# Prompt attention of a hybrid decoder step: the two heads of a pair take turns on TensorE, and the copies of the turned probabilities are dealt anew to ScalarE and VectorE

## The reference, cut to what matters

```python
lc = einsum('bqgrd,bcgd->bgrqc', qg, kc) * scale + t5_bias(dist_c)     # compressed keys
o_c = softmax(lc) @ vc
ls = einsum('bqgrd,bgqmd->bgrqm', qg, ks_sel) * scale + bias_s          # selected blocks
o_s = softmax(ls) @ vs_sel
lw = einsum('bqgrd,bkgd->bgrqk', qg, kw) * scale + t5_bias(dist_w)      # window of 512
o_w = softmax(lw) @ vw
o_n = g[0] * o_c + g[1] * o_s + g[2] * o_w
lf = einsum('bqhd,bkhd->bhqk', q_f, kf) * scale + decay                 # FoX
o_f = softmax(lf) @ vf
```

## Time and profile before

| | |
|---|---|
| Runs | 1849.51, 1849.75, 1855.73 us; median 1849.75 |
| Profiled execution | 1857.19 us, of which span 1855.5 us |
| Busy in the span | PE 1732.8 us (93%), DVE 1057.7 (57%), ACT 696.7 (38%), POOL 300.3 (16%) |
| TensorE clock granted, mean | 0.970 of full speed |
| Prompt attention, first scores to last transposes of the outputs | 575.96 to 990.01 us of the span |

### The profile page before, as it was taken

How to read it: one execution, slowest core, us unless ns; L and a number is a source line. 1 busy time by engine, 2 the same in 40 slices (tenths; PEclk the granted TensorE clock), 3 DMA queues, 4 the chain that set the end, 5 groups by cost and what they waited for, 6 DMA issues and landing times. The chain is left out here.

```text
span 1855.5 us, 35458 instructions
## 1 busy us (share of the span) xinstructions
PE 1732.8 (93%) x13557; PEld 1583.8 (85%) x13557; DVE 1057.7 (57%) x2057; ACT 696.7 (38%) x1369; POOL 300.3 (16%) x629
## 2 busy tenths in 40 slices
PE   7999998899885999998898999999999999999998
PEld 6999998776563777777786879999999999999998
DVE  4533332125354777777776557775666664666665
ACT  4110011223232666565666552133333333344343
POOL 3000023500511434353432000000000000000000
PEclk9999999899896999999998999999999999999998
DMA  5548886645999002030201224132222225231112
GB/s 140 185 133 192 223 231 118 221 137 179 309 318 276 2 20 85 1 103 1 92 2 40 93 87 129 58 99 76 70 90 72 70 71 186 103 125 54 46 42 104
DMA packets 145683, 212.64 MB, mean 115 GB/s; under 512 B 23850, under 2 KB 102105, under 8 KB 145459
## 3 DMA queue, kind: packets, MB, share of 16 engines
q1 hardware_dynamic: 113714, 143.36, 24.3%
q0 software_dynamic: 16480, 52.41, 9.3%
q10 hardware_dynamic: 15328, 14.72, 3.3%
HBM read 163.11 MB, written 51.49 MB: 116 GB/s over the span
## 5 line engine op out<-in xcount | busy, mean ns | idle before, releaser
L2108 ACT ACTIVATE probs<-psum,neg_max 128x640 f32<-128x640 f32 (+7 forms) x192 | 138.2, 720 | 115.5 <-DVE neg_max L2256 114.8
L191 PE MATMUL psum<-h_parts,down_hi 128*128 128x352 f32 x528 | 171.7, 325 | 6.0 <-DVE h_parts L3253 4.4
L191 PE MATMUL psum<-x_hi,w_hi 128*128 128x352 f32 x528 | 170.7, 323 | 1.7 <-issue 1.6
L193 PE MATMUL psum<-h_parts,down_lo 128*128 128x352 f32 x528 | 170.5, 323 | 0.0
L192 PE MATMUL psum<-h_parts,down_hi 128*128 128x352 f32 x528 | 170.5, 323 | 0.0
L192 PE MATMUL psum<-x_lo,w_hi 128*128 128x352 f32 x528 | 170.4, 323 | 0.0
L193 PE MATMUL psum<-x_hi,w_lo 128*128 128x352 f32 x528 | 170.3, 323 | 0.0
L191 PE MATMUL psum<-hf_hi,op_hi 128*128 128x264 f32 x576 | 163.5, 284 | 0.6 <-DVE silu L3234 0.6
L193 PE MATMUL psum<-hf_hi,op_lo 128*128 128x264 f32 x576 | 163.5, 284 | 0.0
L192 PE MATMUL psum<-hf_lo,op_hi 128*128 128x264 f32 x576 | 163.3, 284 | 0.0
L2030 PE MATMUL psum<-ident,probs 128*128 128x128 f32 x848 | 139.1, 289 | 8.9 <-ACT probsT L2118 6.1
(11 more groups left out here) (444 smaller groups left out, 4289.6 us busy)
## 6 DMA issues: line engine op xcount, KB each, us to landing
fox_ring<-in_cache_fox_kv SPq DMA_DIRECT2D x128, 256.0 KB, 5.3
zT<-z_stage SPq DMA_DIRECT2D x22, 528.0 KB, 3.9
w_ring<-in_w_in POOLq DMA_DIRECT2D x22, 512.0 KB, 5.7
down_ring<-in_w_ffn_down SPq DMA_DIRECT2D x44, 256.0 KB, 2.7
raw<-in_w_ffn_gate SPq DMA_DIRECT2D x9, 1024.0 KB, 7.8
raw<-in_w_ffn_up SPq DMA_DIRECT2D x9, 1024.0 KB, 5.4
h_dram<-stage POOLq DMA_DIRECT2D x8, 1056.0 KB, 6.0
nsa_page<-in_cache_nsa_kv POOLq DMA_DIRECT2D x64, 128.0 KB, 6.3
```

The lines of the kernel that those rows point to most:

```text
L191: nc.tensor.matmul(dst, w_hi, x_hi, start=start, stop=False, skip_group_check=onto)
L193: return nc.tensor.matmul(dst, w_lo, x_hi, start=False, stop=stop, skip_group_check=onto)
L2108: nc.scalar.activation(probs[:, u % 4, 0:n], slot_of(u), ACT.Exp, bias=neg_max[:, u % 4:u % 4 + 1], scale=1.0, accum_out=denom[:, m % 2, a ...
```

## The change

Four edits, all in `build_c` and its tables.

1. PE: a round was scores of both heads, transposes of head 0, values, transposes of head 1, `natural`, `mix`. It becomes scores and transposes of head 0, scores and transposes of head 1, `natural`, `mix`, values.
2. ACT: a round was exponent of head 0, copies of head 0, exponent of head 1, the copy to `outT`, copies of head 1. It becomes copies then exponent of head 0, copies of head 1, the copy to `outT`, exponent of head 1.
3. DVE: the copies of head 0 move between the two maxima, those of head 1 right behind the second, ahead of `high_part`.
4. Dealing: the first entry of each unit (tiles 0 to 3) goes to ACT, the second (tiles 4 and up) to DVE. DVE's copies go from 118 to 96, of which 16 instead of 59 are of 512 columns; ACT's from 178 to 200, of which 128 instead of 85.

```diff
-ENTRY_ON = ["AVAVA"[g % 5] for g in range(len(ENTRIES))]
+ENTRY_ON = ["V" if at else "A" for u, at, n in ENTRIES]
...
                 for p in ROUNDS:
-                    for u in pair_of(p + 1):
-                        if u >= 2:
-                            pe.wait_ge(exp_done, u - 1)
-                        scores(u)
-                    for u in pair_of(p)[:1]:
-                        pe.wait_ge(exp_done, u + 1)
-                        turn(u)
-                    if 0 <= p - 1 < NP:
-                        values(p - 1)
-                    for u in pair_of(p)[1:]:
-                        pe.wait_ge(exp_done, u + 1)
-                        turn(u)
+                    for e in range(2):
+                        for u in pair_of(p + 1)[e:e + 1]:
+                            if u >= 2:
+                                pe.wait_ge(exp_done, u - 1)
+                            scores(u)
+                        for u in pair_of(p)[e:e + 1]:
+                            pe.wait_ge(exp_done, u + 1)
+                            turn(u)
                     if p - 2 in ENDS:
                         natural(ENDS[p - 2])
                     if p - 3 in ENDS:
                         mix(ENDS[p - 3])
+                    if 0 <= p - 1 < NP:
+                        values(p - 1)
...
+                    for u in pair_of(p)[:1]:
+                        copies(u)
                     for u in pair_of(p + 1)[:1]:
                         exponent(u)
-                    for u in pair_of(p)[:1]:
+                    for u in pair_of(p)[1:]:
                         copies(u)
-                    for u in pair_of(p + 1)[1:]:
-                        exponent(u)
                     if p - 1 in ENDS:
                         macro = ENDS[p - 1]
                         act.wait_ge(summed, summed_through(last_pair(macro)))
                         CLOSE_ACT.done(nc.scalar.copy(outT[:, macro % 2].rearrange("p k n -> p (k n)"), outs), ("out", macro))
-                    for u in pair_of(p)[1:]:
-                        copies(u)
+                    for u in pair_of(p + 1)[1:]:
+                        exponent(u)
...
                 for p in ROUNDS:
-                    for u in pair_of(p + 1):
-                        peak(u)
+                    for e in range(2):
+                        for u in pair_of(p + 1)[e:e + 1]:
+                            peak(u)
+                        for u in pair_of(p)[e:e + 1]:
+                            for g in entries_of(u):
+                                if ENTRY_ON[g] == "V":
+                                    copy(g)
...
-                    for u in pair_of(p):
-                        for g in entries_of(u):
-                            if ENTRY_ON[g] == "V":
-                                copy(g)
```

## The result

The changed kernel takes 1838.8 us (median of five runs, 1835.0 to 1841.5); the kernel before, run beside it, 1855.6 us (1849.5 to 1860.5). The ratio is 0.992, 95% interval 0.9893 to 0.9947.

A forecast was written before the change was run, and what follows sets the result against it. PE, busy 93% of the span, was taken as the bound, with 40 us of idle time and lowered clock recoverable. Terms -6.8 - 8.6 + 1.0 + 1.4 = -13.0 us gave 1844.2 profiled, 1837 as median; forecast case 1829 to 1844, range 1823 to 1853.

The forecast's parts named there:

- The dealing: Copies dealt anew between ACT and DVE: neither engine becomes the bound; zero, or 1 us either way.
- The cmp places: Three stretches from cmp to win6: waits give 0.1 us, the clock staying up gives 6.7; term -6.8 us.
- The change of head pair: Stretches from win6 to slc2: the fox scores' wait for POOL goes and the clock recovers; term -8.6 us.
- The outT copy: On ACT ahead of the second exponent: PE waits 0.1 to 0.7 us for fox1 to fox7, 11 us in all.
- Full stretches, first and last: From slc2 to cmp, plus head pairs 0 and 3: outT copies and uncovered mix cost +1.0 us.
- Changes of the array's form: Alternating scores and transposes at cmp pairs adds two changes each, 4 x 2 x 0.17: +1.4 us.
- the clock does not come back: Rival: the 10.2 us of clock in the forecast gain are not won; 1847 us, no change; chance 0.22.
- All waits merely change their names: Rival: the change does nothing, ring waits being few and waits only passing elsewhere; 1850 us; chance 0.08.
- Copies first: At the cmp places, copies ahead of exponents on ACT remove the 2.13 us wait of slc5 transposes for a ring place.
- my condition (no wait over 1.3 us): In the cmp stretches the granted clock stays up because no single wait is over 1.3 us, against 2.13 before.

The follow-up runs named there:

- run 5: The changed kernel with the old dealing (A, V, A, V, A over the entries) and all new orders: 1850.5 us, ratio 0.9998, stage 406.82 us.
- run 1: The kernel before with the new dealing alone, all orders old: 1844.1 us, ratio 0.9952, stage 400.56 us.
- run 7: The kernel before, old orders, with all copies of transposed tiles on ACT: stage 402.39 us; 1861.3 us, including a 16.7 us wait in an untouched stage.
- run 8: The kernel before, old orders, with the new dealing mirrored (first four tiles of each unit to DVE, the rest to ACT): stage 420.04 us.
- run 11: Run 4's kernel plus mix behind the values, weighing and POOL's factor first, second cmp head's denominators behind the next pair's first maximum: 1821.2 us, ratio 0.9829.
- run 3: The kernel before with PE's new order alone: ratio 1.0221, stage 447.68 us.
- run 2: The kernel before with ACT's new order alone: 1900.9 us in one run, stage 458.64 us.
- run 4: The changed kernel with ACT's outT copy moved behind the second exponent of the next pair (the outT-last kernel): 1828.2 us, ratio 0.9866, stage 387.72 us.
- run 12: Run 11's kernel with the scores of both cmp heads in one go: 1821.3 us, ratio 0.9832, stage 379.43 us.
- run 6: The changed kernel with DVE's old order (its copies behind both maxima): 1863.0 us in one run, stage 420.72 us.
- run 10: Run 4's kernel with DVE's weighing ahead of its casts and POOL's factor ahead of its low part: 1838.5 us in one run, clock 0.95, time not compared.

## Why the prediction was right in the sum and wrong in its parts

That the time came out 2 us beside the forecast is partly luck. Two errors of opposite sign stood in the sum: by run 5 the orders without the dealing gain 7.2 us in the stage, not 13.0, and the dealing, put at nothing, brings the larger part. And the 1837 us rest on a median of 1849.75 for the kernel before, which took 1855.6 beside the result. (Two small sums of the prediction are off, which changes nothing: the chain behind outT adds up to 1.57 us, the waits at the change of head pair to 5.1.)

*The dealing: zero. Wrong, the step that failed.* It measures 13.3 to 13.5 us by the profiles, two thirds of the 20.5. I compared busy shares over nine stretches, found that ACT has room, and asked only whether a copy between the two maxima is covered. I did not ask what the copies delay. At the cmp place DVE's maxima, copies and denominators stand in one chain that the exponents wait for, and a full-width copy on DVE holds it up by 0.59 us (from 752.60 in run 1 to 753.19 in the earlier trace rows). The sign was there: in the earlier trace rows an exponent waits 1.77 us for DVE. Runs 1, 5, 7 and 8 show it from four sides.

*The cmp places: -6.8. Measured -4.8, but the cause was wrong.* I gave it to the copies first on ACT. The orders without the dealing (run 5) gain 0.7 there and lose the clock in two of three stretches. The dealing alone brings -8.0: by PE's busy time 6.1 of it is clock (6.7 forecast for a clock that stays up, right in size), 1.9 idle time. With the orders on top, 3.2 are given back, but not as idle time. At the cmp place of head pair 2 the two waits of the dealing alone, 1.47 and 1.55 us, become five: 0.48 for the second cmp exponent (0.9 forecast), 0.36 for `natural` (not forecast), 0.15 before the fox5 scores (two of 0.5 forecast), 0.84 and 0.48 for the weighing and `mix` (1.3 forecast), 0.7 less in all. It is PE's busy time that rises, from 18.85 to 20.41 us at the full clock. A wait hides a part of itself there, as the outT copy below shows, and two more changes of form per stretch add to it; how the rise divides between the two is not shown. Run 11 ends with 63.81 us for the three, under the 65.29 of the dealing alone.

*The change of head pair: -8.6. Measured -10.8, right.* The dealing has 1.0 of it, the orders 9.8. The 1.59 us for POOL are gone; what is left, 0.32 at fox0 and 0.64 at slc1 in idle time, some 1.4 with the parts that idle time hides (see the outT copy), is near the 1.3 that I kept. It is PE's order that takes the POOL waits away: run 3, which has it alone, keeps one (3.6 us), runs 1 and 2, which lack it, have four (5.9 and 6.5 us).

*The outT copy: +11. Right in mechanism, and near in size at its places; taking it away gives back less.* Run 4 gains 5.8, or 7.4 without the fall of the clock. The chain for fox7 of head pair 1 after:

```profile
772.96 0.66 PE L2057 MATMUL psum<-probsT,v_fox 128*64 128x128 f32 x8
...
773.66 0.59 ACT L2141 COPY outT<-psum 128x512 f32<-128x512 f32 x1 [0.34 <-PE psum L2057]
...
774.15 0.80 ACT L2106 ACTIVATE probs<-psum,neg_max 128x640 f32<-128x640 f32 x1
...
775.09 0.33 PE L2021 MATMUL psum<-k_parts,high_fox 128*128 128x128 f32 x1 [0.53 <-ACT probs L2106]
```

Copy to exponent 0.49, exponent 0.80, as forecast (0.48, 0.79). The idle time that the last row shows, 0.53, is less than what PE loses: it counts only from the modelled end of the matmul before, and where nothing is waited for the next matmul starts sooner than that. The same four transposes and the scores behind them at fox3 of head pair 1, first after, then with outT last (run 4):

```profile
718.68 0.60 PE L2030 MATMUL psum<-ident,probs 128*128 128x128 f32 x4
719.41 0.42 PE L2021 MATMUL psum<-k_parts,high_fox 128*128 128x320 f32 x1
```

```profile
716.55 0.60 PE L2030 MATMUL psum<-ident,probs 128*128 128x128 f32 x4
716.90 0.39 PE L2021 MATMUL psum<-k_parts,high_fox 128*128 128x320 f32 x1
```

Neither shows idle time, yet from start to start it is 0.73 us and 0.35: the scores come 0.38 us late. Measured so, the second scores of fox1 to fox7 come 0.17, 0.27, 0.38, 0.51, 0.40 (0.62 in head pair 3), 0.73 and 0.77 us late (0.1 to 0.7 forecast), 13.1 us over the stage; in run 4 3.1 are left. So the edit wins 10 us there. The clock took 1.6 of them, and `natural` waits 1.2 longer for DVE copies (2.2 us against 1.0); the rest of the difference to 5.8 is not traced.

*Full stretches, first and last: +1.0. Wrong sign:* -1.2, -2.1 and -1.6 us. The dealing again: alone it gives -1.4, -1.9 and -1.2, while the orders alone (run 5) give +1.3, -0.1 and +0.7.

*Changes of the array's form: +1.4. Not borne out as a cost of time.* The gaps before weight loads that wait for nothing shown are 164 before and 160 after, 29.6 and 31.7 us; and where run 12 takes two changes away, PE's work shrinks by 0.31 us and a wait takes up the time. So the price is there in PE's work (0.17 forecast for a change), but it was covered by the wait. The rule on a drain at each change of mode (the Trainium skill, "TensorEngine Tiling (Array Packing)", Key Properties) agrees with the gap of 0.17 us in front of each group of another form; what it costs depends on the wait behind it.

*The rivals.* The clock came back in all nine stretches, so "the clock does not come back" is out for the change as a whole; with the old dealing it holds at two of the three cmp places (run 5). "All waits merely change their names" is false in sum, yet it is what happens to each edit by itself (runs 3, 6, 10, 12). "Copies first" was never a part that could act alone: with ACT's or PE's order alone, or DVE's left out, the stage is 33.6 and 44.6 us longer than before, and 27.2 longer than after.

What stays open: how far the clock's part belongs to the dealing, since each kernel has one profiled execution. In cmp stretches the clock fell in 7 of 12 with the old dealing (before, runs 2, 3, 5) and in 1 of 21 with the new (run 10 left out). The runs give a bound, an estimate across kernels that ran on different chips: of the executions whose granted clock was 0.977 in the mean of the whole program, those of before took 1848.6 to 1849.8 us, of the dealing alone 1840.8, 1840.9 and 1846.0, of after 1835.0 and 1838.8. So 3 to 9 us of the dealing's gain and 10 to 15 of the change's come at an equal clock.

## What to carry to other kernels

Ask of every engine what its queue delays, not how busy it is: DVE at 57% was late exactly where the exponents waited for it, and moving copies off it was the better half of this change, at no cost that shows. A ring of few places ties the orders of all engines that fill and empty it: change them together, or the stall moves into the ring. When a wait is removed, read who is behind it, and test the edits together: `mix`, weighing and denominators gave 8.3 us as a set (5.8 by `mix` alone, 1.6 of that clock), while the one on weighing alone only moved its wait. And measure a wait of TensorE from start to start against a place without it: the idle time of the profile leaves a part of it out.

## What the runs showed of the hardware

The granted clock does not go by the longest wait. In the mirrored dealing the three cmp stretches hold the same wait of 3.3 us for a DVE copy, and two keep the full clock:

```profile
642.82:666.71 23.89, 19.17 (x198) 16.53 (x197) 22.23 (x66) 9.55 (x25) 8.09 (x18) 1.00 0.01 2
...
745.27:769.08 23.81, 19.15 (x197) 16.50 (x197) 22.15 (x66) 9.55 (x25) 9.01 (x20) 1.00 0.00 1
...
848.88:874.14 25.26, 20.60 (x197) 17.89 (x197) 22.15 (x66) 9.61 (x25) 9.00 (x20) 0.93 0.01 2
```

In the outT-last kernel it fell in the last of the three cmp stretches (lines in run 4), whose waits equal those of the one before, none over 0.84 us. So my condition (no wait over 1.3 us) neither holds it up nor brings it down by itself. A fall costs 1.4 to 1.6 us, by twins with and without: 25.26 less 23.81 and 24.54 less 22.92.

A DVE product of 128x4 takes 0.69 us while POOL works on two operands in SBUF and 0.16 when POOL rests (run 10, at 659.10). In the outT-last kernel:

```profile
745.45 0.73 POOL L2169 TENSOR_TENSOR q_nsa<-q_nsa,high_nsa 128x256 fp32r<-128x256 f32 x1 [9.65 <-DVE high_nsa L2300]
745.51 0.69 DVE L2285 TENSOR_TENSOR factor<-factor,gf_nat 128x4 f32<-128x4 f32 x1
```

Of the 32 such products in the kernel after, 28 meet no POOL work and take 0.16 us; the four beside POOL take 0.42 once and 0.69 three times. The Trainium skill, "GPSIMD Engine Reference", section Specifications, says that the two engines share their interfaces to SBUF and contend when DVE has two inputs there; the trace agrees.
